# Ten in_b tiles and half of out_even moved between RWKV's matmuls, in plain fp32

## The chip, the core and the metric

One core of one Trainium2 chip runs the whole program. The metric is the device time of one execution in microseconds (us); the median of three runs of the kernel before is 3572.96 us (3570.43 to 3578.23).

## The reference, cut to what matters

The program is one inference step of a two-layer recurrent decoder on T = 320 token columns (a prompt of 256 and eight sequences of 8), D_MODEL = 2048, everything float32. Only layer 0's mixer is touched:

```python
def even_mixer(h, lb, s_hgrn, s_rwkv, s_shift, p, j):
    z = jnp.einsum('btd,de->bte', h, p['w_in_even'][j])       # 2048 x 7424
    z_a, z_b = z[..., :4 * D_A], z[..., 4 * D_A:]             # HGRN2 | RWKV-7
    ...                                                        # o_a: chunked_gated_linear
    prev = jnp.concatenate([s_shift[:, None, :].astype(z_b.dtype), z_b[:, :-1]], axis=1)
    zs = z_b + (prev - z_b) * p['rwkv_mu'][j]                  # token shift
    r, kb, v, wl, al, gl = split_cols(zs, [D_B, D_B, D_B, R_W, R_A, R_G])
    ...                                                        # o_b: rwkv7_scan, group norm, gate
    o = jnp.concatenate([o_a, o_b], axis=-1).astype(h.dtype)
    out = jnp.einsum('bte,ed->btd', o, p['w_out_even'][j])
```

The token shift, and with it all of RWKV, needs the columns z_b; the output projection is a sum over an HGRN half (rows 0 to 1023 of the weights) and an RWKV half.

## The kernel before, in words

Activations lie transposed: 128 features on the partitions, 320 tokens along a row. A projection is a list of tiles of 128 output features; a tile has 16 weight blocks of 128x128, streamed from HBM in two units of eight blocks (512 KB). The order is in_a (32 tiles: HGRN's q, f, i, g), in_b (26 tiles: RWKV's r, k, v and the low-rank inputs), out_even (16 tiles), then the SwiGLU projections and the odd layer, which the change leaves alone.

**Split matmuls.** Every projection is computed in float32r on split operands. ACT rounds a unit's weights to `w_hi` (`split_hi`, L283), DVE or POOL subtracts to get `w_lo` (`split_lo`, L291), and `multiply_unit` (L326) issues three matmuls a block: x_hi and x_lo with w_hi (L348), x_hi with w_lo (L352). The raw weights pass through a ring of four buffers, loaded by SP (`ring_load`, L270), and w_hi and w_lo have two buffers each. In in_b the subtraction is POOL's, elsewhere DVE's.

**HGRN stage.** HGRN2 works through four groups of two heads (`hgrn_act`, `hgrn_dve`, `hgrn_pe`). A group has 21 numbered stages: a head (gates, cumulative log decay), eight levels in which DVE, ACT, PE and DVE hand on to each other (differences L815 and L816, exponentials, products L830 and L831, small Gram matmuls L931 to L937, selects), and a tail (transposes, outputs L957, states L963, sum of squares L974, reciprocal L886, products L981). in_b runs in between: `fill_pe` puts one unit of in_b (24 matmuls) into PE's program at every 1.5 stages, `fill_act` splits and evicts, and `in_b_pool` on POOL subtracts and then applies the token shift to each finished tile (`shift_pool`, nine operations and a memset, L1058 to L1069). `by_stage` (L639) merges such programs by their stage numbers into one program per engine, in which each engine then goes strictly in order.

**RWKV stage.** RWKV-7 runs in two passes; in each, two groups of two head pairs go side by side (`rwkv_act`, `rwkv_dve`, `rwkv_pool`, `rwkv_pe` with x = 0 and 1; buffers in `RwkvBuffers`, L1002). A pass has 74 stages: low-rank projections and norms (0 to 8), transposes and Grams (8 to 16), five rounds of a block-triangular inverse (17 to 36, L1408, L1416, L1418), five chunk steps (37 to 63, L1446 to L1471), the sampled states (65 to 68), group norm and gate (68 to 74). Group x has the PSUM banks 4x to 4x+3. No projection runs beside it.

**out_even.** After the last RWKV group, `mixer_x_act` and `x_lo_dve` split the eight parts of the mixer's output, and out_even runs as 32 units with `evacuate` (L361) and `squares_act` (L407) behind each tile. HGRN's buffers (`hK` and on, L649) lie in the region of M; M held the weighted input `xw` before and takes out_even's result.

Of the kernel before, what the change touches and what calls it, by code (L numbers as in the profile page):

```python
# [17 lines left out]
P = 128  # L18
# [91 lines left out]
def build(nc, d):  # L110
# [5 lines left out]
    with ctx:  # L116
# [126 lines left out]
        FILL = {0: 0, "mix0": 1, 2: 2, 4: 3, "mix1": 4, 6: 5}  # L243
        LEADS, MIXES = {0: 0, 2: 1, 3: 2, 5: 3}, {1: 0, 4: 1}
# [58 lines left out]
        def lead_unit(pe, s, xh, xl, fill):  # L303
# [5 lines left out]
            pe.wait_ge(sem("x_hi"), 8 * fill + c + 1)  # L309
# [16 lines left out]
        def multiply_unit(pe, i, s, xh, xl, fill=None):  # L326
# [9 lines left out]
            half, tile = n % 2, g.tile0 + n // 2  # L336
# [3 lines left out]
            out = PS[tile % 4][:, 0:T]  # L340
            for k in range(g.kt):
                kk = half * g.kt + k
                if fill is not None and not g.lead and n < 2 and kk % 2 == 0:
                    c = kk // 2
                    pe.wait_ge(sem("x_hi"), 8 * fill + c + 1)
                    pe.wait_ge(sem("x_lo_mix"), 8 * MIXES[fill] + c + 1)
# [4 lines left out]
            for k in range(g.kt):  # L351
                mm = nc.tensor.matmul(out, w_lo[s % 2][:, k, :], xh[:, half * g.kt + k, :], start=False,  # L352
                                      stop=half == 1 and k == g.kt - 1)
# [7 lines left out]
        def evacuate(dve, g, out, accumulate=False, stats=None, skip=0, after=None):  # L361
# [19 lines left out]
            def tile_out(i, s):  # L381
# [25 lines left out]
        def squares_act(act, g, stats, w, after, skip=0):  # L407
# [12 lines left out]
            def body(i, s):  # L420
# [3 lines left out]
                if n >= 3 and n % 2:  # L424
                    t = (n - 3) // 2
# [4 lines left out]
            act.activation(warm[:, :], rms_eps, ACT.Sqrt).then_inc(sem("root_table"), 1)  # L430
# [49 lines left out]
        rs = stat[:, 1, :]  # L480

# [12 lines left out]
        def boundary_act(act, n, g, fill, w):  # L494
            if n is not None:
                root_act(act, n)
            for c in range(8):
                if n is None:
                    act.wait_ge(sem(f"x_in{c}"), 16)
# [11 lines left out]
        def boundary_dve(dve, n, g, fill):  # L511
# [5 lines left out]
            for c in range(9):  # L517
# [6 lines left out]
                if c and g is not None:  # L524
                    dve.wait_ge(sem("x_hi"), 8 * fill + c)
# [42 lines left out]
        def mixer_x_act(act):  # L568
            for c in range(8):
# [79 lines left out]
        hK = at("hK", HT0, [P, HG, T])  # L649
        hB = at("hB", HT0 + 2560, [P, HG, T])  # L650
        hEa = at("hEa", HT0 + 5120, [P, HG, T])
        hXa = at("hXa", HT0 + 7680, [P, HG, T])
        hV = at("hV", HT0 + 10240, [P, 3, HG, P])
        hN = at("hN", HT0 + 13312, [P, 3, HG, P])
        att0 = at("att0", HT0 + 16384, [P, HG, 256])
        att1 = at("att1", HT0 + 18432, [P, HG, 128])
        att2 = at("att2", HT0 + 19456, [P, HG, 64])
        hS = at("hS", HT0 + 25728, [P, HG, SEQS, P])
        hVM = at("hVM", HT0 + 19968, [P, SEQS, P])
        hgm_in = at("hgm_in", HT0 + 19968, [P, 8, 128], i32)  # L660
# [31 lines left out]
        def fill_stage(u):  # L692

            return u * (HGROUPS * HSTAGES - 6) // plan["in_b"].units

        def fill_act(act):
            g = plan["in_b"]
            yield 0
            split_hi(act, 0, g.unit0)
            for u in range(g.units + 1):  # L700
                yield fill_stage(u) + (u == g.units)
                if u + 1 < g.units:
                    split_hi(act, 0, g.unit0 + u + 1)
# [1404 lines left out]
```

## Time and profile before

| what | value |
|---|---|
| median of three runs | 3572.96 us |
| the profiled execution's own time | 3568.65 us |
| its span, first to last instruction | 3566.6 us |
| mean granted TensorE clock | 0.957 |
| PE busy, share of the span | 3352.9 us, 94% |
| DVE, ACT, POOL busy | 1917.7, 1253.8, 460.1 us |
| read from HBM | 450.66 MB, 133 GB/s over the span |

Times are from one execution taken by the hardware profiler. "Busy" of PE counts each matmul from its issue to its modelled end, so that matmuls in a pipeline overlap and a busy PE need not be at its peak. A plain fp32 matmul leaves two records, a split one leaves one. The granted clock is 1.00 at 2.4 GHz and 0.50 at 1.2 GHz.

### The profile page before, as it was taken

What the parts mean: (1) busy time and instruction counts of PE and PEld (TensorE: products, weight loads), DVE (VectorE), ACT (ScalarE), POOL (GpSimd) and SP (SyncE); (2) the same over time, 40 slices, a digit from 0 to 9 for tenths busy, and PEclk for the clock granted to TensorE, in tenths of its full rate; (3) what the DMA queues carried; (4) which work ended last, traced back from release to release, by engine and by line L of the source; (5) the groups of instructions that cost most, each with busy time, mean ns of one, the idle gap of its engine ahead of it and who ended that gap; (6) DMA issues with size and microseconds to landing.
All of it is one profiled execution on the core that took longest, in us unless ns stands there. A gap on an engine that the chain in (4) does not pass through costs nothing.

```text
span 3566.6 us, 61189 instructions
## 1 busy us (share of the span) xinstructions
PE 3352.9 (94%) x24672; PEld 3239.9 (91%) x24672; DVE 1917.7 (54%) x2317; ACT 1253.8 (35%) x1582; POOL 460.1 (13%) x400
## 2 busy tenths in 40 slices
PE   8998896858899999999999999998999999999997
PEld 8998885847889999999999899986989999999997
DVE  5446667584566454355544666924475543455444
ACT  5344343232353332233333435321453332233332
POOL 0018774000000000000000035920000000000000
PEclk9999997979899999999999999986999999999999
DMA  6443331000444454454444544533444444445543
GB/s 200 150 143 108 120 108 56 3 26 16 147 131 148 147 150 155 138 151 147 149 159 142 194 147 120 172 137 136 147 130 148 147 154 153 135 147 152 157 146 110
DMA packets 118662, 474.88 MB, mean 133 GB/s; under 512 B 13425, under 2 KB 15089, under 8 KB 115569
## 3 DMA queue, kind: packets, MB, share of 16 engines
q1 hardware_dynamic: 108864, 421.58, 38.4%
q10 hardware_dynamic: 9648, 51.17, 3.7%
q8 instruction: 112, 1.84, 0.2%
q14 instruction: 38, 0.30, 0.0%
HBM read 450.66 MB, written 22.03 MB: 133 GB/s over the span
## 4 chain that ended last, share of the span: by engine, by line
PE 88%; DVE 7%; ACT 2%; issue 1%; POOL 1%; DMA 0%; ACTq 0%; DVEq 0%; POOLq 0%
PE ps L348 49%; PE ps L352 25%; PE ps L1842 1%; PE ps L312 1%; PE ps L317 1%; PE ps L322 1%; PE ps L1862 1%; PE ps L1416 1%; PE ps L957 1%; PE ps L1418 1%; PE ps L1380 0%; PE ps L1365 0%; PE ps L935 0%; PE ps L1597 0%; DVE hEa L886 0%
## 5 line engine op out<-in xcount | busy, mean ns | idle before, releaser
L348 PE MATMUL ps<-x_hi,w_hi 128*128 128x320 f32 x4768 | 1424.1, 312 | 39.9 <-DVE x_lo L548 28.7
L288 ACT ACTIVATE w_hi<-raw 128x1024 fp32r<-128x1024 f32 (+1 forms) x756 | 842.0, 1114 | 1741.3 <-PE ps L352 1688.4
L348 PE MATMUL ps<-x_lo,w_hi 128*128 128x320 f32 x4768 | 1415.6, 310 | 0.0
L296 DVE TENSOR_TENSOR w_lo<-raw,w_hi 128x1024 fp32r<-128x1024 f32 (+1 forms) x640 | 834.5, 1306 | 788.3 <-ACT w_hi L288 775.7
L348 PEld LDWEIGHTS ps<-x_hi,w_hi 128*128 128x128 f32 x4768 | 902.1, 189 | 48.3 <-issue 30.7
L348 PEld LDWEIGHTS ps<-x_lo,w_hi 128*128 128x128 f32 x4768 | 902.1, 189 | 0.9
L352 PE MATMUL ps<-x_hi,w_lo 128*128 128x320 f32 x4768 | 800.9, 310 | 11.4 <-POOL w_lo L296 11.2
L352 PEld LDWEIGHTS ps<-x_hi,w_lo 128*128 128x128 f32 x4768 | 726.1, 189 | 15.2 <-POOL w_lo L296 14.3
L296 POOL TENSOR_TENSOR w_lo<-raw,w_hi 128x1024 fp32r<-128x1024 f32 x116 | 302.8, 2616 | 1682.2 <-ACT w_hi L288 1680.4
L348 PE MATMUL ps<-u_hi,w_hi 128*128 128x320 f32 x1408 | 416.6, 310 | 8.3 <-DVE u_lo L610 8.3
L348 PE MATMUL ps<-u_lo,w_hi 128*128 128x320 f32 x1408 | 416.1, 310 | 0.0
L348 PEld LDWEIGHTS ps<-u_hi,w_hi 128*128 128x128 f32 x1408 | 265.2, 188 | 9.3 <-DVE u_lo L610 9.3
L348 PEld LDWEIGHTS ps<-u_lo,w_hi 128*128 128x128 f32 x1408 | 265.2, 188 | 0.0
L352 PE MATMUL ps<-u_hi,w_lo 128*128 128x320 f32 x1408 | 227.3, 309 | 0.0
L352 PEld LDWEIGHTS ps<-u_hi,w_lo 128*128 128x128 f32 x1408 | 211.7, 188 | 0.0
L601 DVE TENSOR_TENSOR stat<-ps,stat 128x320 f32<-128x320 f32 x88 | 43.3, 492 | 110.3 <-PE ps L352 110.3
L597 DVE TENSOR_TENSOR gate<-ps,stat 128x320 f32<-128x320 f32 x88 | 43.2, 491 | 95.4 <-PE ps L352 95.3
L373 DVE COPY M<-ps 128x320 f32 (+1 forms) x64 | 31.5, 492 | 110.5 <-PE ps L352 110.5
L312 PE MATMUL ps<-x_hi,w_hi 128*128 128x320 f32 x256 | 47.3, 331 | 33.0 <-ACT x_hi L506 33.0
L312 PEld LDWEIGHTS ps<-x_hi,w_hi 128*128 128x128 f32 x256 | 42.4, 205 | 34.4 <-issue 34.4
L371 DVE TENSOR_TENSOR Z<-ps,stat 128x320 f32 (+1 forms) x48 | 22.8, 489 | 52.5 <-PE ps L352 52.5
L369 DVE TENSOR_TENSOR M<-ps,M 128x320 f32 (+1 forms) x32 | 15.7, 492 | 65.3 <-PE ps L352 65.3
(374 smaller groups left out, 2902.9 us busy)
## 6 DMA issues: line engine op xcount, KB each, us to landing
raw<-in_w_ffn_in SPq DMA_DIRECT2D x352, 512.0 KB, 3.6
raw<-in_w_ffn_out SPq DMA_DIRECT2D x128, 704.0 KB, 4.1
raw<-in_w_in_even SPq DMA_DIRECT2D x116, 512.0 KB, 3.6
raw<-in_w_in_odd SPq DMA_DIRECT2D x96, 512.0 KB, 3.6
raw<-in_w_out_even SPq DMA_DIRECT2D x32, 512.0 KB, 3.6
raw<-in_w_out_odd SPq DMA_DIRECT2D x32, 512.0 KB, 3.6
hS<-in_state_hgrn ACTq DMA_DIRECT2D x4, 1024.0 KB, 4.9
out_hgrn_s<-hS ACTq DMA_DIRECT2D x4, 1024.0 KB, 5.1
```

The source lines that it names most:

```text
L288: nc.scalar.activation(w_hi[s % 2][:, 0:g.kt, :], raw[s % 4][:, 0:g.kt, :], ACT.Copy)\
L296: eng.tensor_tensor(w_lo[s % 2][:, 0:g.kt, :], raw[s % 4][:, 0:g.kt, :], w_hi[s % 2][:, 0:g.kt, :].bitcast(f32), sub).then_inc(sem(f"split ...
L312: nc.tensor.matmul(out[t], w_hi[s % 2][:, 4 * kk + t, :], xh[:, 2 * c + kk, :], start=c == kk == 0, stop=False)
L317: nc.tensor.matmul(out[t], w_hi[s % 2][:, 4 * kk + t, :], xl[:, 2 * c + kk, :], start=False, stop=False)
L322: mm = nc.tensor.matmul(out[t], w_lo[s % 2][:, 4 * kk + t, :], xh[:, 2 * c + kk, :], start=False, stop=c == 7 and kk == 1)
L348: nc.tensor.matmul(out, w_hi[s % 2][:, k, :], x[:, kk, :], start=half == 0 and k == 0 and x is xh, stop=False)
L352: mm = nc.tensor.matmul(out, w_lo[s % 2][:, k, :], xh[:, half * g.kt + k, :], start=False, stop=half == 1 and k == g.kt - 1)
L597: dve.tensor_tensor(gate[:, p % 2, :], bank_of(g, 2 * p)[:, 0:T], rs, mult)\
L601: dve.tensor_tensor(uf, bank_of(g, 2 * p + 1)[:, 0:T], rs, mult).then_inc(sem("tile_out"), 1)
L957: ins = mm(o[:, a:a + 8], hS[:, j, b, :], hQ[:, j, 8 * b:8 * b + 8], start=False, stop=b == 7)
L1416: ins = mm(bank[2 + n // 8][a:b, o], r.T1[a:b, n], r.XT[a:b, n], start=True, stop=True)
L1418: ins = mm(bank[n // 8][a:b, o], r.XT[a:b, n], r.T1[a:b, n], start=True, stop=True)
```

## The change

in_b leaves the split scheme. Its 26 tiles are reordered (`IN_B`: those of the first RWKV pass first) and computed as plain fp32 matmuls from the raw weights and the unsplit input `xw`, 16 a tile instead of 48. Sixteen tiles run in the HGRN stage, in chunks of four matmuls; ten run in RWKV's first pass, in chunks of three or four. In RWKV's second pass run the 16 tiles of out_even's HGRN half, eight matmuls each in chunks of 3, 3 and 2, and ACT copies them to M. out_even itself keeps the RWKV half: one unit per tile, added to M. All of this in RWKV uses bank 7, so that group x = 1 has three banks, and some of its rows are cut in two pieces of 192 and 128 columns. The weights of these tiles come through three buffers in the space of the ring, which is loaded again only when the last of them is used. POOL has no weights to split any more; it shifts sixteen tiles in HGRN and ten in RWKV, the latter evicted and scaled by DVE. HGRN's buffers move to the space of x_hi and x_lo, since `xw` has to stay. Smaller parts: the input's eight loads become four, and the subtraction of the mean in RWKV's group norm moves ahead of the state updates on DVE.

```diff
-        dense("in_b", d["w_in_even"], 26, KU_MODEL, "pool", 32)
-        dense("out_even", d["w_out_even"], KT, KU_MODEL, "dve")
+        dense("out_even", d["w_out_even"], KT, KU_MODEL, "dve", 8, 1)
...
             def body(i, s):
                 if s >= 4:
                     split_wait(sp, i, s - 4)
+                if g is plan["out_even"] and s - g.unit0 == 2:
+                    rbuf[1].wait(sp, "ys", 10)
...
+        FILL_H, FILL_B, FILL_O = 16, len(IN_B), KT
+        fraw = [at(f"fraw{i}", RAW0 + 4 * KU_MODEL * P * i, [P, KU_MODEL, P]) for i in range(3)]
+
+        def fill_load(sp):
+            sp.wait_ge(sem("split_lo_dve"), plan["in_a"].units)
+            for u in range(2 * FILL_B + FILL_O):
+                if u >= 3:
+                    sp.wait_ge(sem("fill_unit"), u - 2)
...
+            sp.wait_ge(sem("fill_unit"), 2 * FILL_B + FILL_O)
+
+        def fill_matmul(p, bank, m):
+
+            kt = KU_MODEL
+            u, k = (2 * p + m // kt, m % kt) if p < FILL_B else (FILL_B + p, m)
+            if k == 0:
+                nc.tensor.wait_ge(sem(f"fill_in{u % 3}"), 16 * (u // 3 + 1))
+            last = 2 * kt - 1 if p < FILL_B else kt - 1
+            mm = nc.tensor.matmul(bank, fraw[u % 3][:, k, :], xw[:, m, :] if p < FILL_B else Z[:, m, :],
+                                  start=m == 0, stop=m == last)
...
+        X_IN = (0, 1), (1, 2), (2, 4), (4, 8)
...
-        def fill_stage(u):
-
-            return u * (HGROUPS * HSTAGES - 6) // plan["in_b"].units
+        def fill_stage(p, m):
+
+            return (32 * p + 2 * m) * (HGROUPS * HSTAGES - 2) // (32 * FILL_H)
 
         def fill_act(act):
...
+            for p in range(FILL_H):
+                yield fill_stage(p + 1, 0) + 1
+                fill_done(act, p)
+                act.activation(Z[:, IN_B[p], :], PS[p % 4][:, 0:T], ACT.Copy).then_inc(sem("fill_out"), 1)
 
         def fill_pe(pe):
...
+            for p in range(FILL_H):
+                for m in range(0, 16, 4):
+                    yield fill_stage(p, m)
+                    if m == 0 and p >= 4:
+                        pe.wait_ge(sem("fill_out"), p - 3)
+                    for k in range(m, m + 4):
+                        fill_matmul(p, PS[p % 4][:, 0:T], k)
...
+        def fill_at(p):
+
+            return 6 * (p - FILL_H) if p < FILL_B else RSTAGES + 4.5 * (p - FILL_B)
...
+        def shift_late(pool):
+            for p in range(FILL_H, FILL_B):
+                yield fill_at(p) + 6
+                shift_pool(pool, p)
+
+        def rwkv_fill_pe(pe):
+            for p in range(FILL_H, FILL_B + FILL_O):
+                cuts = (0, 3, 6, 9, 12, 16) if p < FILL_B else (0, 3, 6, 8)
+                for i, (a, b) in enumerate(zip(cuts, cuts[1:])):
+                    yield fill_at(p) + i
+                    if a == 0:
+                        pe.wait_ge(sem("fill_out"), p)
+                    for m in range(a, b):
+                        fill_matmul(p, PS[7][:, 0:T], m)
+
+        def rwkv_fill_dve(dve):
+
+            for p in range(FILL_H, FILL_B):
+                yield fill_at(p) + 5
+                fill_done(dve, p)
+                dve.tensor_tensor(Z[:, IN_B[p], :], PS[7][:, 0:T], rs, mult).then_inc(sem("fill_out"), 1)
+
+        def rwkv_fill_act(act):
+            for p in range(FILL_B, FILL_B + FILL_O):
+                yield fill_at(p) + 3
+                fill_done(act, p)
+                act.activation(M[:, p - FILL_B, :], PS[7][:, 0:T], ACT.Copy).then_inc(sem("fill_out"), 1)
...
-                self.bank = PS[4 * x:4 * x + 4]
+
+                b = self.bank = PS[4 * x:4 * x + (4, 3)[x]]
...
+                    self.row1 = [(b[2][:, T:512], slice(0, 192)), (b[1][:, T:T + 128], slice(192, T))]
...
+                yield at0 + 66
+                w("mu", G + 1)
+                for j in range(RJ):
+                    for ps, ts in r.row(j):
+                        ins = dve.tensor_tensor(r.Y[:, j, ts], r.Y[:, j, ts], ps, sub)
+                ins.then_inc(r.sem("yc"), 1)
                 for j in range(RJ):
                     yield at0 + (66 if j == 0 else 68)
...
-            by_stage(rwkv_act(act, 0), rwkv_act(act, 1))
+            by_stage(rwkv_act(act, 0), rwkv_act(act, 1), rwkv_fill_act(act))
...
-            mixer_x_act(act)
+            mixer_x_act(act, 4)
...
-            by_stage(rwkv_dve(dve, 0), rwkv_dve(dve, 1))
+            by_stage(rwkv_dve(dve, 0), rwkv_dve(dve, 1), rwkv_fill_dve(dve))
...
-            evacuate(dve, plan["out_even"], M, stats=0, skip=HEAD, after=plan["up00"])
+            evacuate(dve, plan["out_even"], M, accumulate=True, stats=0, skip=HEAD, after=plan["up00"])
...
-            by_stage(rwkv_pe(pe, 0), rwkv_pe(pe, 1))
+            by_stage(rwkv_pe(pe, 0), rwkv_pe(pe, 1), rwkv_fill_pe(pe))
```

## Rows read from the trace of the kernel before

**Rows 1.** The chain of work that ended last: shares of the span by engine.
```profile
PE 88%; DVE 7%; ACT 2%; issue 1%; POOL 1%; DMA 0%; ACTq 0%; DVEq 0%; POOLq 0%
```
**Rows 2.** Busy time by stretch (HGRN, RWKV, out_even); columns: length, engines, clock, DMA.
```profile
core 0: us, PE busy (x) PEld busy (x) DVE busy (x) ACT busy (x) POOL busy (x), PEclk, DMA share, GB/s
239.70:586.60 346.90, 309.59 (x1892) 280.06 (x1890) 234.17 (x338) 142.02 (x203) 264.10 (x312) 0.92 0.33 105
586.60:904.90 318.30, 222.30 (x4136) 189.51 (x4136) 201.67 (x326) 84.93 (x191) 6.48 (x4) 0.82 0.06 20
904.90:1022.00 117.10, 112.65 (x750) 112.68 (x751) 58.28 (x70) 51.74 (x72) 0.00 (x0) 0.96 0.53 163
```
**Rows 3.** Timeline of out_even: first matmul of two units in succession.
```profile
915.54 0.31 PE L348 MATMUL ps<-x_hi,w_hi 128*128 128x320 f32 x1
...
919.06 0.31 PE L348 MATMUL ps<-x_hi,w_hi 128*128 128x320 f32 x1
```
**Rows 4.** Chain in order of time: eight fp32 matmuls 128x128x320 in a row.
```profile
2133.58 4.31 PE ps L1597 x16
```
**Rows 5.** Busy time in HGRN: third group's head, levels and tail; the fourth group.
```profile
411.50:429.40 17.90, 14.64 (x92) 14.25 (x90) 5.15 (x10) 13.44 (x17) 10.02 (x13) 0.90 0.69 260
429.40:470.70 41.30, 37.33 (x238) 34.92 (x237) 35.15 (x57) 13.21 (x22) 35.98 (x42) 0.92 0.27 77
470.70:501.60 30.90, 30.06 (x168) 26.31 (x167) 17.06 (x16) 9.86 (x16) 23.48 (x30) 0.89 0.31 88
501.60:586.60 85.00, 71.44 (x413) 61.52 (x411) 57.65 (x83) 31.33 (x46) 62.78 (x85) 0.86 0.27 88
```
**Rows 6.** Timeline of DVE in the third group's levels.
```profile
433.67 2.52 DVE L815 TENSOR_TENSOR hEa<-hB 128x320 f32<-128x320 f32 x1
436.11 2.66 DVE L816 TENSOR_TENSOR hEa<-hB 128x320 f32<-128x320 f32 x1
...
455.93 0.41 DVE L815 TENSOR_TENSOR hEa<-hB 128x256 f32<-128x256 f32 x1
```
**Rows 7.** Timeline of POOL at the same time.
```profile
432.79 5.63 POOL L296 TENSOR_TENSOR w_lo<-raw,w_hi 128x1024 fp32r<-128x1024 f32 x2
```
**Rows 8.** Timeline of PE in the third group: one level, then the tail.
```profile
456.99 1.05 PE L935 MATMUL ps<-hXa 128*128 128x128 f32 x8
...
477.08 2.59 PE L957 MATMUL ps<-hQ,hS 128*128 128x8 f32 x16
...
485.70 1.98 PE L963 MATMUL ps<-hVM,hN 64*128 64x512 f32 x4
...
491.23 1.24 PE L974 MATMUL ps<-Z,com 128*128 128x320 f32 x4
```
**Rows 9.** Busy time in RWKV's first pass, and the end of the second.
```profile
591.70:621.50 29.80, 10.36 (x32) 5.81 (x32) 25.06 (x34) 12.68 (x22) 3.21 (x2) 0.61 0.09 30
621.50:645.90 24.40, 19.63 (x300) 18.70 (x300) 20.19 (x38) 7.78 (x20) 0.00 (x0) 0.92 0.01 1
645.90:684.50 38.60, 33.84 (x994) 33.17 (x995) 22.38 (x38) 6.65 (x14) 0.00 (x0) 0.87 0.01 4
684.50:713.00 28.50, 26.85 (x618) 25.77 (x619) 4.75 (x15) 6.95 (x26) 0.00 (x0) 0.95 0.01 3
713.00:747.00 34.00, 21.25 (x140) 11.76 (x137) 26.22 (x34) 5.96 (x12) 0.00 (x0) 0.80 0.14 51
...
869.00:904.90 35.90, 19.51 (x141) 11.25 (x140) 27.21 (x36) 6.04 (x12) 0.00 (x0) 0.79 0.09 34
```
**Rows 10.** Timeline of PE in RWKV: two groups of four small matmuls at clock 1.00.
```profile
664.27 0.33 PE L1418 MATMUL ps<-T,XT 64*64 64x64 f32 x4
...
664.39 0.33 PE L1416 MATMUL ps<-XT,T 64*64 64x64 f32 x4
```
**Rows 11.** Timeline of POOL: first and last of one tile's ten shift instructions.
```profile
475.08 0.85 POOL L1058 TENSOR_TENSOR Z<-Z,stat 128x320 f32<-128x320 f32 x1
...
478.46 0.86 POOL L1069 TENSOR_TENSOR Z<-Z,shd 128x320 f32<-128x320 f32 x1
```

More of the change, by code:

```diff
@@ L335, in multiply_unit @@
             pe.wait_ge(sem("split_hi"), i * 8 + (s + 1))
-            half, tile = n % 2, g.tile0 + n // 2
+            half, tile = (n % 2, g.tile0 + n // 2) if g.parts == 2 else (0, g.tile0 + n)
             if half == 0 and tile >= 4 and not (g.lead and n < 14):
@@ L340, in multiply_unit @@
             out = PS[tile % 4][:, 0:T]
+            k0 = half * g.kt if g.parts == 2 else g.kt
             for k in range(g.kt):
[L342 to L346, printed above, removed]
+                kk = k0 + k
+                if fill is not None and not g.lead and n < g.parts and kk % 2 == 0:
+                    c = kk // 2 if g.parts == 2 else k // 2
+                    pe.wait_ge(sem("x_hi"), fill + c + 1)
+                    pe.wait_ge(sem("x_lo_mix"), MIXES[fill] + c + 1)
                 for x in (xh, xl):
@@ L351, in multiply_unit @@
             for k in range(g.kt):
-                mm = nc.tensor.matmul(out, w_lo[s % 2][:, k, :], xh[:, half * g.kt + k, :], start=False,
-                                      stop=half == 1 and k == g.kt - 1)
+                mm = nc.tensor.matmul(out, w_lo[s % 2][:, k, :], xh[:, k0 + k, :], start=False,
+                                      stop=half == g.parts - 1 and k == g.kt - 1)
             mm.then_inc(sem("unit_done"), 1)
@@ L388, in tile_out @@
                         one(0, t, g.unit0 + 2 * t + 2)
+                elif g.parts == 1:
+                    one(0, n, s + 1)
                 elif n % 2 and not (g.lead and n < 12):
@@ L566, in mixer_part, with mixer_x_act @@
             return Z[:, z:z + 2, :]
-        def mixer_x_act(act):
-            for c in range(8):
+        def mixer_x_act(act, first=0):
+            for c in range(first, 8):
                 act.activation(part(x_hi, c), mixer_part(c), ACT.Copy).then_inc(sem("x_hi"), 1)
@@ L1395, in rwkv_pe @@
                 w("gm", 5 * G + 3)
-                gram(4, 2, bank[2]).then_inc(r.sem("n4"), 1)
+                for c in range(4 if x else 0):
+                    ins = gram(c, 2, r.n03[:, 64 * RJ * c:64 * RJ * c + 64 * RJ])
+                    if c == 3:
+                        ins.then_inc(r.sem("n03"), 1)
+                if x:
+                    w("gm", 5 * G + 4)
+                gram(4, 2, r.n4).then_inc(r.sem("n4"), 1)
                 for l in range(1, 6):
@@ L1893, in _ @@
             for name in ORDER:
+                if name == "out_even":
+                    fill_load(sp)
                 ring_load(sp, plan[name])
@@ L2054 @@
     w_odd_units = units(np.concatenate([qk, w_odd[:, 2048:]], axis=1), KU_MODEL)
+    in_even, out_even = units(a["w_in_even"][0], KU_MODEL), units(a["w_out_even"][0], KU_MODEL)
+    in_b = [b + j for b in (R_B, K_B, V_B) for j in range(4)] + [WA_B, GL_B] + \
+           [b + j for j in range(4, 8) for b in (R_B, K_B, V_B)]
+    in_even = np.concatenate([in_even[:64]] + [in_even[2 * t:2 * t + 2] for t in in_b])
     dram = {
```

248 lines of the change are left out of this document (137 added, 111 removed).

## Prediction

> **What bounds the kernel now.** I read the chain of waits first: PE's share of it is 88% [rows 1], so what counts is how long PE's program takes, its own waiting included. Then the busy time by stage [rows 2]: the change touches three stages, HGRN with in_b (346.9 us), RWKV (318.3 us) and out_even (117.1 us). out_even is PE without a gap. In HGRN all of PE, DVE and POOL are busy over two thirds of the time; in RWKV PE shows 222 of 318 us at a mean granted clock of 0.82, and nothing but RWKV's own chain runs there. Then the pace of the two kinds of matmul. A split unit of 24 matmuls takes 919.06 - 915.54 = 3.52 us [rows 3], 0.147 us each and 0.440 us for the three that a weight block needs. Eight plain fp32 matmuls of the same shape (16 records) take 4.31 us [rows 4], 0.539 us each. So fp32 is dearer for PE by 0.099 us a block, and cheaper only for those who split.
>
> PE's work by these paces: in_b 416 blocks x 0.440 = 183.0 us and out_even 256 x 0.440 = 112.6 us before; after it 256 x 0.539 = 138.0 us in HGRN, (160 + 128) x 0.539 = 155.2 us in RWKV and 128 x 0.440 = 56.3 us in out_even. PE gets 54 us more work. The change wins only if RWKV hides much of its 155 us and HGRN shrinks by the lighter load.
>
> **HGRN.** A middle group takes 90 us: head 17.9, levels 41.3, tail 30.9 [rows 5]. Its fills were 13 units, 45.8 us of PE; they become 4 tiles, 34.5 us, in chunks of 4 x 0.539 = 2.16 us instead of units of 3.52 us.
>
> Levels. DVE's six large operations of a level take 0.41 us each where nothing disturbs them, 2.5 us a level; but single ones show 2.5 to 2.7 us [rows 6], for as long as POOL's subtractions of w_lo run [rows 7]. Those are gone with the change. A level's Gram takes PE 1.05 us [rows 8]; with a handover I take 1.2. A stage with a chunk then costs 2.16 + 1.2 + 0.1 = 3.4 us, one without is DVE's 2.5; there are 64 chunks in 82 stages, so 0.78 x 3.4 + 0.22 x 2.5 = 3.2 us a stage. The first three levels also carry the sequences: 3.7. That is 5 x 3.2 + 3 x 3.7 + 3 for the ends = 30, with 1.5 for POOL's shifts 31.5: 9.8 us less than now. The same sum with a unit of 3.52 us at two stages of three gives 37 of the 41 seen; the rest is POOL.
>
> Tail. From the end of the outputs L957 at 479.7, units stand ahead of L963 (485.70) and L974 (491.23) [rows 8]; the first ran at half clock. Chunks there instead shorten 21.8 us to about 17.2: 4.6 us less. The head is DMA and table loads; I take 0.5 us off for the split that ACT no longer does. So two middle groups gain 14.9, the first, with a shorter head, 13; the last, whose tail had hardly any fill (85.0 us), 9.5: **HGRN -52 us**. If DVE and PE still wait for each other at every stage, a group gains only 6, 24 us in all; if the stalls all go and chunks fall into DVE's time, 20, 80 us in all.
>
> **RWKV.** Own sum by window [rows 9], chunks by the stage numbers in the diff; a chunk of three is 1.62 us, an in_b tile 8.62 us.
> - 591.7 to 621.5 (stages 0 to 8): 11.9 us of chunks, PE idle 19.4: DVE is the bound. Hidden but for the chunk ahead of the first low-rank matmuls, 3.2 us at half clock, and an eviction: +4.
> - 621.5 to 645.9: 14.0 us of chunks, 4.8 idle, 1 back from the clock (0.92 granted; the chunks keep PE at it): +8.
> - 645.9 to 684.5, the inverse: 27.5 us of chunks, 4.8 idle, and 4 back from the clock (0.87: 10 us at half): +18.7.
> - 684.5 to 713, the chunk steps: 32.9 us of chunks. PE shows 26.85 busy of 28.5, but four records take 664.39 - 664.27 = 0.12 us [rows 10], so 618 records are 18.5 us of work and the rest their latency. Between 1.7 and 10 us idle I take 7, nearer the pace since the two groups alternate: +25.9.
> - 713 to 747: no chunks. The mean is subtracted before the state updates: -2.
>
> First pass +54.6. The second pass has windows within 2 us of these and 16 tiles of 4.31 us, 69.0 us, spread to stage 144: 8.6, 8.6, 18.9, 21.6 and 11.3 us by window, of which I hide 7.6, 5.1, 8, 6 and 10 (the last window's PE is idle for 16.4): +32. Unseen costs: PE's change between 64x64 and full tiles at 98 chunks (0 to 0.25 us each, a handover like the 0.1 above); x = 1 with three banks (four more ACT or DVE pieces a pass, 0 to 0.4 us each; no gain but the -2 above); ten shifts on POOL beside RWKV's DVE. I take +5 for them together, near the low end, since most fall where PE has other work. **RWKV +92 us**, so 155 - 92 = 63 us hidden. From below: all idle of the windows used, +75; from above: only the DVE-bound windows at the starts of the passes hide anything, 155 - 20 - 10 of clock = +125.
>
> New waits. PE waits for bank 7's eviction before each tile; queued behind are all RWKV matmuls. In the first window that eviction stands on DVE behind two long reciprocals, but so do the transposes. ACT's 16 copies and DVE's 10 evictions (0.4 to 0.5 us) wait for chunks that PE runs before what they need next. SP's loads are 84 units of 512 KB before and after; three buffers leave two units (8.6 us) for a landing. The four merged input loads are covered by the 20 us before their last parts are used; uncovered, some us once.
>
> **out_even** loses 384 split matmuls: -56 us (54 to 58). DVE's add to M costs what its copy did; two tiles instead of one finish behind the last unit, below 1 us.
>
> **Sum:** -52 + 92 - 56 = -16 us. The sum is against the profiled execution, 3568.65 us, which lies 4.3 below the median shown, 3572.96; I forecast the median: **3557 us**.
>
> **The rivals.**
> - *Forecast*, 0.45: RWKV +82 to +100, HGRN -45 to -60; 3540 to 3570, within 0.2% of before in a fifth of it. (0.2%, 7 us, is about what a measurement of this kernel can tell from no change.)
> - *HGRN was held by POOL*, 0.24: POOL is busy for 36 of the levels' 41 us [rows 5]; without its lock-outs and with finer chunks a group goes to 70 us. HGRN -80: 3529. Against it: the last group lost four units of fill and gained only 5 us.
> - *A chunk is a step of RWKV's chain*, 0.16, slower: PE goes strictly in order, so both groups' next step stands behind each chunk even where DVE or ACT would have been waited for anyway only for a moment; from the inverse on nothing is hidden. RWKV +125: 3573 + 17 = 3590. It decides once RWKV grows by more than 52 + 56 = 108 us. For it: PE shows 27 of 28.5 us in the chunk steps. Against: the pace in rows 10.
> - *POOL locks DVE out in RWKV*, 0.06, slower: a shift takes 479.3 - 475.1 = 4.2 us [rows 11], 3.4 without its first operation; ten of them are 34 us beside a DVE that is the bound in three windows. All of it on the path: -16 + 34 - 2 = +16, 3589. In HGRN's levels DVE's 35.2 busy us exceed its undisturbed 24 by 11, a third of POOL's 36, which would make it 10. The Trainium skill (SBUF — State Buffer, "SBUF: two separate sides") has a rule for this: GpSimd and a VectorE operation with two SBUF inputs share a port pair as an exclusive lock, and the loser waits out the whole instruction. By that rule the full 34 us could come due; the trace agrees that a stalled operation ends with POOL's, and shows that most meet none.
> - *HGRN does not shrink*, 0.05, slower: its chain of handovers, not the fills, sets the pace, so the lighter load does nothing. -20 instead of -52: 3589.
> - *A wash*, 0.04: the errors cancel; 3573.
>
> **How the numbers follow.** Faster: 0.36 of the forecast and the second case, 0.60. Same: 0.09 + 0.04 + 0.03 from the edges of the slower ones, 0.16. Slower: 0.24. The range goes from somewhat below the second case (RWKV a little better with it) to just above 3590: 3515 to 3592. The likeliest case's own range is 3540 to 3570.
>
> **What would show it.** Right: HGRN's groups at 74 to 77 us, DVE operations in the levels at 0.4 to 0.5 us; RWKV at 400 to 415 us with PE's clock near 1.00 from the transposes to the chunk steps; out_even's matmuls half as many in half the time. Wrong: groups still at 85 us; RWKV over 425 us, with DVE and ACT waiting for PE at every step of the inverse and the chunk steps; DVE operations of 1 us beside POOL's shifts on the chain; PE waiting for bank 7 or for a weight load.

## The result: 0.46% slower, and the profile after

The changed kernel takes 3589.84 us (median of seven runs, 3583.56 to 3596.86), the kernel before 3573.35 beside it: 1.0046 times as long, 95% interval 1.0033 to 1.0059. One of the seven runs of the kernel before, 4055.29 us, was slow and does not enter the ratio. The forecast was 3557 and faster; the time lies inside the range, on the wrong side.

The profiled execution took 3584.75 us, 16.1 more than that of before. I cut both traces at marks that both kernels have (first moved matmul, last mark of HGRN, last write of RWKV's gate, first transpose and end of the odd layer's retention stage); times in us:

| stretch | before | after | predicted | measured |
|---|---|---|---|---|
| to the first in_b matmul | 240.2 | 238.5 | 0 | -1.7 |
| HGRN | 346.5 | 280.4 | -52 | -66.1 |
| RWKV | 318.1 | 448.1 | +92 | +130.0 |
| out_even, up to the retention stage | 1438.4 | 1383.0 | -56 | -55.4 |
| retention stage (code not touched) | 139.2 | 148.4 | 0 | +9.2 |
| from there to the end | 1084.3 | 1084.7 | 0 | +0.4 |

So up to the retention stage the change comes to +6.8 (-1.7 of it ahead of HGRN), 0.2% of the time; between a second profile of each kernel, below, it is +3.6. The larger part of the 16.1 is a stage 1400 us later. The same stretches by busy time (HGRN, RWKV, out_even), which answer to [rows 2]:

```profile
core 0: us, PE busy (x) PEld busy (x) DVE busy (x) ACT busy (x) POOL busy (x), PEclk, DMA share, GB/s
238.00:518.80 280.80, 259.24 (x1152) 185.84 (x1152) 166.51 (x338) 89.13 (x142) 73.02 (x150) 0.92 0.29 93
518.80:967.00 448.20, 389.54 (x4728) 294.40 (x4728) 209.89 (x341) 92.05 (x210) 47.20 (x104) 0.90 0.19 58
967.00:1030.60 63.60, 58.54 (x384) 58.31 (x384) 37.47 (x53) 32.73 (x52) 0.00 (x0) 0.93 0.55 176
```

HGRN's POOL time fell from 264 to 73 us and its DVE time from 234 to 167 us. In RWKV PE is busy for 167 us more, DVE and ACT for 8 and 7 each, POOL for 41: the 130 us are PE's, or POOL's by way of DVE.

**HGRN after.** DVE's timeline in a level of the third group, against [rows 6]: nothing of 2.5 us is left.

```profile
402.22 0.41 DVE L858 TENSOR_TENSOR hEa<-hB 128x256 f32<-128x256 f32 x1
402.56 0.41 DVE L859 TENSOR_TENSOR hEa<-hB 128x256 f32<-128x256 f32 x1
```

PE's timeline in the same levels: a chunk and a Gram follow each other without a gap, 412.29 - 409.24 = 3.05 us a stage. In these levels PE now sets the pace.

```profile
409.24 2.32 PE L310 MATMUL ps<-M,fraw 128*128 128x320 f32 x8
411.40 1.05 PE L978 MATMUL ps<-Z 128*128 128x128 f32 x8
412.29 2.32 PE L310 MATMUL ps<-M,fraw 128*128 128x320 f32 x8
```

**RWKV after.** Busy time by stage: start, transposes and Grams, inverse, chunk steps with the sampled state, end; the first pass, then the second. Read the PE column against the length: in rows 2 to 4 and 7 to 9 PE is busy for 94% or more, at the starts and ends of the passes for half to two thirds.

```profile
518.90:557.70 38.80, 24.55 (x80) 16.00 (x80) 28.30 (x40) 16.74 (x28) 11.75 (x21) 0.74 0.26 85
557.70:594.00 36.30, 34.31 (x352) 27.90 (x352) 23.00 (x41) 7.68 (x20) 3.80 (x10) 0.95 0.15 45
594.00:655.30 61.30, 60.21 (x1095) 48.53 (x1094) 23.53 (x41) 6.64 (x14) 14.11 (x36) 1.00 0.20 62
655.30:724.60 69.30, 69.04 (x811) 53.62 (x810) 7.45 (x21) 8.32 (x30) 12.06 (x35) 0.93 0.22 63
724.60:754.20 29.60, 18.57 (x74) 8.99 (x74) 26.51 (x37) 4.55 (x7) 2.26 (x3) 0.88 0.16 56
754.20:783.30 29.10, 16.53 (x54) 10.62 (x54) 26.38 (x40) 14.87 (x26) 3.22 (x2) 0.73 0.20 58
783.30:813.70 30.40, 29.48 (x334) 24.89 (x334) 20.19 (x38) 8.56 (x22) 0.00 (x0) 0.92 0.06 19
813.70:869.40 55.70, 52.91 (x1064) 43.41 (x1064) 23.04 (x39) 8.40 (x18) 0.00 (x0) 0.97 0.17 50
869.40:933.40 64.00, 63.84 (x793) 49.72 (x792) 6.97 (x20) 10.79 (x36) 0.00 (x0) 0.92 0.15 45
933.40:967.00 33.60, 20.12 (x81) 10.72 (x80) 24.45 (x32) 5.41 (x9) 0.00 (x0) 0.83 0.25 94
```

PE's timeline at the first chunk step shows how: two groups' products of 0.6 us stand between runs of six and seven moved matmuls. Six matmuls hold PE for 659.35 - 655.92 = 3.43 us, against 6 x 0.539 = 3.23 back to back: 0.2 a run for the change between small and full tiles. The Trainium skill (TensorEngine Tiling (Array Packing), "Key Properties") says that changing the tiling mode drains the engine; these rows agree in that 0.2 us a run is lost, though no row shows a drain itself.

```profile
655.31 0.68 PE L1563 MATMUL ps<-nat,G 64*64 64x64 f32 x16
655.92 3.50 PE L310 MATMUL ps<-M,fraw 128*128 128x320 f32 x12
659.35 0.68 PE L1573 MATMUL ps<-RH,XT 64*64 64x64 f32 x16
659.96 4.04 PE L310 MATMUL ps<-M,fraw 128*128 128x320 f32 x14
```

### The profile page after: what moved, and what is told of

It is laid out like the page before. It is cut to its first block, busy times and chain, and to the rows that moved or that the text cites. A ratio compares the mean times of both kernels' runs of the same rounds, so it can differ in the third digit from the quotient of the medians.

```text
span 3583.0 us, 59330 instructions
## 1 busy us (share of the span) xinstructions
PE 3423.4 (96%) x24144; PEld 3198.2 (89%) x24144; DVE 1835.8 (51%) x2313; ACT 1188.1 (33%) x1518; POOL 308.7 (9%) x338
## 4 chain that ended last, share of the span: by engine, by line
PE 91%; DVE 6%; ACT 2%; DMA 1%; issue 1%; ACTq 0%; SPq 0%; DVEq 0%
PE ps L390 46%; PE ps L394 23%; PE ps L310 7%; PE ps L1966 1%; PE ps L1986 1%; PE ps L352 1%; PE ps L357 1%; PE ps L362 1%; PE ps L978 1%; PE ps L1533 1%; PE ps L1525 1%; PE ps L1490 1%; PE ps L1721 0%; PE ps L1553 0%; PE ps L1535 0%
## 5 line engine op out<-in xcount | busy, mean ns | idle before, releaser
L390 PE MATMUL ps<-x_hi,w_hi 128*128 128x320 f32 x4224 | 1252.4, 310 | 28.7 <-DVE x_lo L595 27.0
L390 PE MATMUL ps<-x_lo,w_hi 128*128 128x320 f32 x4224 | 1249.7, 309 | 0.0
L390 PEld LDWEIGHTS ps<-x_hi,w_hi 128*128 128x128 f32 x4224 | 794.9, 188 | 32.2 <-issue 28.7
L390 PEld LDWEIGHTS ps<-x_lo,w_hi 128*128 128x128 f32 x4224 | 795.0, 188 | 0.6
L394 PE MATMUL ps<-x_hi,w_lo 128*128 128x320 f32 x4224 | 706.2, 309 | 0.4 <-DVE w_lo L336 0.3
L394 PEld LDWEIGHTS ps<-x_hi,w_lo 128*128 128x128 f32 x4224 | 641.0, 188 | 2.9 <-POOL w_lo L336 1.7
L336 POOL TENSOR_TENSOR w_lo<-raw,w_hi 128x1024 fp32r<-128x1024 f32 x64 | 169.8, 2659 | 1380.3 <-ACT w_hi L328 1380.3
L310 PE MATMUL ps<-M,fraw 128*128 128x320 f32 x832 | 265.0, 470 | 15.5 <-DVE Z L1165 9.8
L310 PEld LDWEIGHTS ps<-M,fraw 128*128 128x128 f32 x832 | 164.5, 205 | 85.7 <-issue 23.7
L310 PE MATMUL ps<-Z,fraw 128*128 128x320 f32 x256 | 81.7, 464 | 0.0
L352 PE MATMUL ps<-x_hi,w_hi 128*128 128x320 f32 x256 | 47.3, 331 | 31.5 <-ACT x_hi L553 31.5
L352 PEld LDWEIGHTS ps<-x_hi,w_hi 128*128 128x128 f32 x256 | 42.4, 205 | 32.9 <-issue 32.9
```

Source lines behind the costliest of these rows:

```text
L310: mm = nc.tensor.matmul(bank, fraw[u % 3][:, k, :], xw[:, m, :] if p < FILL_B else Z[:, m, :], start=m == 0, stop=m == last)
L336: eng.tensor_tensor(w_lo[s % 2][:, 0:g.kt, :], raw[s % 4][:, 0:g.kt, :], w_hi[s % 2][:, 0:g.kt, :].bitcast(f32), sub).then_inc(sem(f"split ...
L352: nc.tensor.matmul(out[t], w_hi[s % 2][:, 4 * kk + t, :], xh[:, 2 * c + kk, :], start=c == kk == 0, stop=False)
L390: nc.tensor.matmul(out, w_hi[s % 2][:, k, :], x[:, kk, :], start=half == 0 and k == 0 and x is xh, stop=False)
L394: mm = nc.tensor.matmul(out, w_lo[s % 2][:, k, :], xh[:, k0 + k, :], start=False, stop=half == g.parts - 1 and k == g.kt - 1)
```

## The experiments

Theory "PE pays": work moved between RWKV's matmuls is free only where PE waited for DVE; elsewhere each matmul costs its 0.54 us and each run of them its change of tile. Rivals: side costs of the move (three banks, evictions, POOL), pieces that delay the chain, and POOL as what held HGRN.

**All of in_b left in HGRN (`e4_hgrn26`).**

```diff
-        FILL_H, FILL_B, FILL_O = 16, len(IN_B), KT
+        FILL_H, FILL_B, FILL_O = len(IN_B), len(IN_B), KT
```

> All 26 tiles of in_b run in HGRN, still in plain fp32 and chunks of four; RWKV's first pass has none; out_even's half stays in the second pass. 'PE pays': HGRN is bound by PE too now, ten tiles of 8.62 us add 75 to 85 us to its 281 (355 to 366), and RWKV's first pass gives back about 80: 3580 to 3600 in all. Rival 'HGRN has room': with POOL's subtractions gone the tiles fall into PE's waits there, HGRN 330 to 345 and the time 3560 to 3575.

Measured: 3567.12 us, 0.9985 (0.9976 to 0.9995) of before. Both HGRN's 337.6 us and the time lie in the range of the rival 'HGRN has room'; 'PE pays' had HGRN at 355 or more. Ten tiles of 86 us add 57, so HGRN hides 29 of them. Its busy time:

```profile
239.60:577.20 337.60, 336.56 (x1472) 244.53 (x1472) 170.34 (x339) 92.72 (x152) 121.13 (x250) 0.96 0.34 108
```

PE's idle time there fell from 21.6 us (280.80 - 259.24) to 1.0, and at a mean granted clock of 0.96 in place of 0.92 some 9 us less are lost (0.08 x 280.8 against 0.04 x 337.6, an estimate): together these are the 29. So the room was PE's own idle time and its clock, and the idle time is used up. RWKV's first pass, now without tiles and still with seven banks:

```profile
577.20:611.30 34.10, 11.69 (x37) 7.53 (x37) 27.01 (x40) 16.90 (x28) 7.32 (x12) 0.68 0.19 66
611.30:636.30 25.00, 20.75 (x302) 19.25 (x302) 20.18 (x38) 7.68 (x20) 0.00 (x0) 0.89 0.01 2
636.30:673.80 37.50, 32.13 (x992) 31.46 (x992) 22.32 (x38) 6.64 (x14) 0.00 (x0) 0.91 0.01 3
673.80:707.50 33.70, 32.05 (x691) 30.84 (x689) 6.43 (x18) 8.37 (x30) 0.00 (x0) 0.87 0.03 7
707.50:737.50 30.00, 19.53 (x80) 9.57 (x76) 25.48 (x37) 4.54 (x7) 0.00 (x0) 0.84 0.15 53
```

The sum is 160.3 us, 161.3 before: the missing fourth bank, the cut rows and the moved mean together cost nothing. Against the changed kernel's first five rows this prices the moved matmuls stage by stage (their count is half the records of L310 in the stretch; a matmul on a boundary counts on both sides, and the three at the end are out_even's):

| stage | without | with | matmuls x 0.539 | cost | predicted |
|---|---|---|---|---|---|
| start | 34.1 | 38.8 | 22: 11.9 | 4.7 | 4 |
| transposes, Grams | 25.0 | 36.3 | 26: 14.0 | 11.3 | 8 |
| inverse | 37.5 | 61.3 | 52: 27.8 | 23.8 | 18.7 |
| chunk steps | 33.7 | 69.3 | 62: 33.2 | 35.6 | 25.9 |
| end | 30.0 | 29.6 | 3: 1.6 | -0.4 | -2 |

In all 75 us, where leaving the ten tiles in HGRN costs 57: the move of the ten tiles loses 18.

**Only the HGRN part**, out_even whole behind RWKV.

```diff
-        FILL_H, FILL_B, FILL_O = 16, len(IN_B), KT
+        FILL_H, FILL_B, FILL_O = len(IN_B), len(IN_B), 0
...
-        dense("out_even", d["w_out_even"], KT, KU_MODEL, "dve", 8, 1)
+        dense("out_even", d["w_out_even"], KT, KU_MODEL, "dve")
...
```

Its out_even reads the weight units in the order in which the changed kernel stores them, by halves, and multiplies them tile by tile, so the layer's output is another sum; the amount of work is that of before.

> Only the HGRN part of the change: all 26 tiles of in_b in plain fp32 in HGRN, nothing between RWKV's matmuls (seven banks stay), out_even whole behind it as before. 'The move is what lost': HGRN 338 as in e4_hgrn26 against 347 before, RWKV 315 to 320, out_even 119 to 121; no slower than the kernel before: 3560 to 3566 with a retention stage of 139 us, 3569 to 3575 with one of 148. 'Plain fp32 is what lost' (a weight block takes PE 0.54 us instead of 0.44): slower than the kernel before, 3580 or more.

Measured: 3552.08 us, 0.9945 (0.9928 to 0.9963); HGRN 334.2, RWKV 313.8, the time below both ranges of 'The move is what lost'. Plain fp32 in HGRN is not what lost: it gains 12 us there although each block costs PE more. Single runs spread from 3543.9 to 3568.6, and the profiled one was the slowest, with a retention stage of 156 us.

**out_even's half only where PE waited.**

In `o_tile` stand a tile's place in PE's program, its bank, the place of ACT's copy and what has to be done with the bank before:

```diff
+        def o_tile(q):
+            G, i = divmod(q - 1, 8)
+            at0 = G * RSTAGES
+            if q == 0:
+                return 0.5, 7, 1.0, None
+            if i < 5:
+                return at0 + 4.2 + i / 10, (7, 0, 1, 4, 7)[i], at0 + (5.5, 6.5, 6.6, 6.7, 8.6)[i], \
+                    (None, (0, "norm"), (0, "norm"), (1, "norm"), None)[i]
+            return at0 + 72 + (i - 5) / 10, (0, 1, 7)[i - 5], at0 + 72 + (i - 5) / 10, \
+                ((0, "sd"), (0, "sd"), None)[i - 5]
...
```

> All of in_b in HGRN as in e4_hgrn26, and out_even's sixteen HGRN-half tiles not spread over RWKV's second pass but set where PE waited in the passes without fills: one before the first low-rank products, five ahead of the transposes and three (two in the second pass) behind the gate of each pass, over the free banks 7, 0, 1 and 4. 'PE pays': a moved matmul is free only where PE waits; the trace of the first pass of e4_hgrn26 shows waits of 5, 17, 7, 5 and 3 us, some 60 us in both passes for 69 us of work. RWKV 327 to 337 instead of 372, the time 3522 to 3532. Rival 'the pieces delay the chains around them': ACT's copies between the exponentials and the low-rank products behind the tiles make each of the four clusters 5 us or more longer than its matmuls' excess: RWKV 350 or more, 3545 or more.

Measured: 3510.32 us (five runs, 3509.32 to 3517.16), 0.9833 (0.9820 to 0.9846): faster than both kernels. RWKV takes 318.0 us, as long as before and 4 us longer than without any moved work (313.8), with all 69 us of out_even's half in it; 327 to 337 were expected. PE's timeline ahead of the transposes: five tiles as one run of 40 matmuls, 0.54 us each.

```profile
591.09 21.70 PE L310 MATMUL ps<-Z,fraw 128*128 128x320 f32 x80
612.63 0.60 PE L1499 MATMUL ps<-com,Z 128*64 128x128 f32 x4
```

and busy time of the first two stages, which answer to the first two rows of the kernel with all in_b in HGRN above:

```profile
574.30:612.60 38.30, 33.81 (x132) 23.25 (x133) 30.14 (x44) 18.64 (x33) 7.35 (x12) 1.00 0.40 130
612.60:635.00 22.40, 18.19 (x301) 17.55 (x299) 17.09 (x31) 8.00 (x21) 0.00 (x0) 0.98 0.09 26
```

The start is 4.2 us longer, since the tiles are more than its waits hold. The transposes and Grams behind it are 2.6 us shorter, at a granted clock of 0.98 in place of 0.89; but most of this is not the clock. DVE's first copy of a transpose, here and in the kernel with all in_b in HGRN:

```profile
613.70 2.61 DVE L1292 COPY nat<-ps 64x256 f32<-64x256 f32 x6 [2.54 <-PE ps L1499]
```

```profile
614.38 1.72 DVE L1268 COPY nat<-ps 64x256 f32<-64x256 f32 x4
```

It comes 1.1 us after the first transpose (612.63) here and 3.1 us after it (611.3) there, where DVE first finishes some 3 us of the second group's products, which the longer start takes over here. That is 2.0 of the 2.6 us.

**An eighth of the moved matmuls.**

```diff
                     for m in range(a, b):
-                        fill_matmul(p, PS[7][:, 0:T], m)
+                        if m % KU_MODEL == KU_MODEL - 1:
+                            fill_matmul(p, PS[7][:, 0:T], m)
...
```

In `fill_matmul` the wait for a unit's weights and the start of a sum move to the matmul that is left.

> Leaves out seven eighths of the moved products in RWKV (one matmul of every eight stays, with its loads, evictions, shifts and the seven banks), so ten in_b tiles and half of out_even are not what they should be. Theory 'PE pays': from the transposes on PE has no time to spare, so every moved matmul costs its 0.54 us, every change between small and full tiles some 0.19 us, and only the waits for DVE at the ends of a pass hide any. Then RWKV falls from 448 us to 318 to 330, and the time to 3462 to 3478. Theory 'side costs': 30 us or more of RWKV's growth come from group x = 1 with three banks, the evictions and POOL's shifts. Then RWKV stays at 345 to 360 and the time at 3490 to 3505. For both: the retention stage, whose code is the same, moves by up to 10 us with the clock granted there.

Measured: 3477.86 us (four runs, 3464.50 to 3492.12), the upper end of the first theory's range; RWKV 339.8, between the two. The first pass without tiles above has settled the banks, so what stays is the pieces: this first pass takes 174.3 us with 20 lone matmuls against 160.3 without, 0.70 us each, which is 0.54 and 0.16 for the change of tile; the second pass gives 0.71 (165.6 with 16, 154.2 in the kernel with only the HGRN part). Even lone matmuls, spread evenly, are not hidden. My figure for the first theory had left these out.

**One piece a tile.**

```diff
-                cuts = (0, 3, 6, 9, 12, 16) if p < FILL_B else (0, 3, 6, 8)
+                cuts = (0, 16) if p < FILL_B else (0, 8)
```

> Every moved tile runs in RWKV as one piece (16 or 8 matmuls) instead of five or three: 26 pieces instead of 98, which stand as 64 uninterrupted runs in the trace. 'PE pays': same matmuls, fewer changes of tile shape, 38 x 0.19 = 7 us less, with a few us of hiding lost: 3580 to 3592. Rival 'a piece is a delay of the chain of both groups': pieces of 4 to 8.6 us in place of 1.6 make each group wait longer than PE could use: 3605 or more.

Measured: 3601.99 us, 1.0088 (1.0071 to 1.0104); RWKV 458.8, 10.7 longer, between the two figures. The first pass's start alone went from 38.8 to 50.8 us. PE's timeline there:

```profile
522.94 11.71 PE L310 MATMUL ps<-M,fraw 128*128 128x320 f32 x32 [5.05 <-ACT Z L1179]
...
558.91 10.82 PE L310 MATMUL ps<-M,fraw 128*128 128x320 f32 x32 [11.55 <-DVE Z L1165]
569.57 1.26 PE L1475 MATMUL ps<-com,Z 128*64 128x128 f32 x10
```

One whole tile, partly at half clock, stands ahead of the low-rank products, where three matmuls do in the changed kernel; the next waits 11.55 us for DVE to empty bank 7 and then stands whole ahead of the transposes. The chunk steps, with fewer pieces, fell from 69.3 to 59.1, the inverse rose from 61.3 to 73.2, together 132.3 against 130.6: there the size of a piece hardly matters.

**RWKV's shifts left out**, but for the two copies of the shift state.

```diff
             if p < FILL_H:
                 L(pool.tensor_tensor(z, z, rs, mult))
+            else:
+                pool.tensor_copy(sh_out[:, n, 0:1], z[:, 255:256])
+                pool.tensor_copy(sh_out[:, n, 1:9], z[:, 263:T:8]).then_inc(sem("shifted"), 1)
+                pool.wait_ge(sem("shifted"), p + 1)
+                return
```

> Leaves out seven of the nine POOL operations of the ten token shifts in RWKV (only the two copies for the shift state stay), so RWKV's second pass works on unshifted columns. 'PE pays': PE sets the pace, DVE's waits behind POOL cost little: 0 to 5 us less, 3585 to 3590. Rival 'POOL locks DVE out in RWKV': ten shifts of about 3 us each come off the path: 25 to 30 us less, 3560 to 3565.

Measured: 3590.11 us, 1.0052 (1.0033 to 1.0070), the same as the changed kernel. RWKV is 3.5 us shorter (444.6), and the retention stage of the profiled run 7.6 longer. That is inside the first theory's 0 to 5. So POOL's shifts have next to no part in RWKV's growth.

**POOL's load put back in HGRN, and taken out of the kernel before.** In the first, `xf` are columns of `xw` and `load_to` is unused space.

```diff
             pool.wait_ge(sem("fill_out"), p + 1)
+            for _ in range(3 if p < FILL_H else 0):
+                L(pool.tensor_tensor(load_to[:, :], xf[:, 0:1024], xf[:, 1024:2048], sub))
```

> The changed kernel with the load on POOL put back in HGRN: three subtractions of 128x1024 for each of the sixteen tiles, on data that nobody uses, some 125 us of POOL in all. 'POOL held HGRN': DVE operations of 2.5 us come back, and HGRN grows from 281 to 300 to 315 us. 'PE pays': PE sets the pace in the levels, DVE has slack for the stalls: HGRN 281 to 290.

Measured: 3642.95 us, 1.0197 (1.0182 to 1.0211); HGRN 335.6 instead of 280.4, beyond the ranges of both theories. DVE's timeline in a level, and POOL's beside it:

```profile
445.00 2.50 DVE L858 TENSOR_TENSOR Z<-hB 128x256 f32<-128x256 f32 x1
447.43 2.56 DVE L859 TENSOR_TENSOR Z<-hB 128x256 f32<-128x256 f32 x1
449.92 2.56 DVE L873 TENSOR_TENSOR hXa<-hK,hEa 128x256 f32<-128x256 f32 x1
```

```profile
444.88 7.32 POOL L1127 TENSOR_TENSOR load_to<-M 128x1024 f32<-128x1024 f32 x3 [9.76 <-ACT Z L747]
```

Three DVE operations of 0.41 us take 2.5 each, one for each of POOL's three, and each ends 0.2 to 0.3 us behind it. The Trainium skill (SBUF — State Buffer, "SBUF: two separate sides") says that the loser of the port pair waits out the whole instruction of the other; these rows agree, 2.44 us (7.32 / 3) being one POOL operation.

The kernel before, with POOL's subtraction cut to one block of eight:

```diff
-            eng.tensor_tensor(w_lo[s % 2][:, 0:g.kt, :], raw[s % 4][:, 0:g.kt, :],
-                              w_hi[s % 2][:, 0:g.kt, :].bitcast(f32), sub).then_inc(sem(f"split_lo_{name}"), 1)
+            kt = 1 if g is plan["in_b"] else g.kt
+            eng.tensor_tensor(w_lo[s % 2][:, 0:kt, :], raw[s % 4][:, 0:kt, :],
+                              w_hi[s % 2][:, 0:kt, :].bitcast(f32), sub).then_inc(sem(f"split_lo_{name}"), 1)
```

> The kernel before, with POOL's subtraction of w_lo in in_b cut to the first of its eight weight blocks, so seven eighths of in_b's low weight parts are stale and its result is not exact; PE, ACT and DVE issue the same instructions as before. 52 operations of 2.7 us become short, some 120 us less of POOL. 'POOL held HGRN': HGRN falls from 347 us to 305 to 320. 'PE pays': PE's own 310 busy us and the handovers set the pace, HGRN 335 to 345.

Measured: 3541.63 us, 0.9905 (0.9888 to 0.9922); HGRN 323.2 instead of 346.5, between the two. So seven eighths of POOL's subtraction cost the kernel before 23 us. Why about the same load costs 55 in the changed kernel, where three operations come in a row, no run settles.

**The retention stage.** Four runs: each kernel again, and each with the stage's first four transposes issued seven times.

```diff
-                for k in range(4):
+                for k in [0, 1, 2, 3] * (7 if m == 0 else 1):
```

> The kernel before, unchanged, for a second profile. If the clock in the retention stage goes with the program, that stage takes 139 us again and the whole 3566 to 3571. If it changes from run to run, the stage takes 148 or 156 us as in the five other profiles, and the time of this run is longer by as much.

> The changed kernel, unchanged, for a second profile: layer 0's mixer within 1 us of the first, and a retention stage of 148 or 156 us. A stage of 139 us would say that the clock there changes from run to run and that the changed kernel has no part in it; the time would then be 3575 to 3578.

> The kernel before, with the first four transposes of the retention stage issued seven times instead of once, 24 x 0.114 = 2.7 us more PE work at the start of the stage and nothing else. 'The stage's place decides which part of it meets the full clock': the stage takes 148 us or more, the time 3581 or more. 'The programs ahead of it decide': 139 + 3 = 142 us, 3575 to 3577.

> The same 2.7 us of repeated transposes in the changed kernel. 'The stage's place decides': its length leaves 148 + 3 by 8 us or more either way. 'The programs ahead of it decide': 151 us, the time 3 us longer than the changed kernel's.

Measured: before again 139.1 us (3574.3 in all), after again 148.4 (3587.19; layer 0's mixer 1.4 us longer than in the first profile). With the 2.7 us of transposes: the kernel before takes 3588.50 us, 1.0037 (1.0027 to 1.0048), its stage 152.9; the changed kernel 3580.45, 1.0020 (1.0010 to 1.0031) of before and 9 us below its own median, its stage 145.9 in the profiled run, which is 2 us shorter than the changed kernel's. The first answers as 'the stage's place' had it; the second lies 5.5 us from the 151 of the other theory, short of the 8 us asked, and fits neither. Busy time of the whole stage, before and after, then cut where the granted clock changes; the kernel before, the changed one, and the longest stretch at half clock of the one before with the transposes:

```profile
2343.10:2482.30 139.20, 129.22 (x512) 92.51 (x512) 53.48 (x70) 24.26 (x44) 0.87 (x1) 0.70 0.29 113
```

```profile
2349.90:2498.30 148.40, 138.41 (x513) 96.10 (x513) 53.55 (x70) 24.32 (x45) 0.83 (x1) 0.65 0.27 106
```

```profile
2343.10:2359.10 16.00, 15.14 (x112) 13.72 (x112) 6.51 (x13) 11.03 (x21) 0.87 (x1) 0.99 0.45 157
2359.10:2376.10 17.00, 17.00 (x70) 15.80 (x69) 0.00 (x0) 0.77 (x2) 0.00 (x0) 0.50 0.24 100
2376.10:2390.10 14.00, 14.00 (x58) 7.81 (x57) 9.50 (x10) 2.41 (x3) 0.00 (x0) 0.98 0.24 99
2390.10:2403.10 13.00, 13.00 (x49) 11.44 (x49) 1.97 (x4) 0.77 (x2) 0.00 (x0) 0.50 0.56 217
2403.10:2417.10 14.00, 14.00 (x59) 7.90 (x59) 9.57 (x10) 1.12 (x2) 0.00 (x0) 0.99 0.26 109
...
2430.10:2444.10 14.00, 14.00 (x59) 7.89 (x60) 9.63 (x10) 0.97 (x2) 0.00 (x0) 0.98 0.26 111
```

```profile
2349.90:2368.90 19.00, 18.18 (x136) 16.66 (x137) 6.51 (x13) 11.03 (x21) 0.83 (x1) 0.99 0.54 204
2368.90:2419.90 51.00, 51.00 (x150) 36.23 (x150) 11.47 (x13) 4.54 (x8) 0.00 (x0) 0.50 0.22 89
2419.90:2432.90 13.00, 13.00 (x56) 7.23 (x54) 9.21 (x10) 0.53 (x1) 0.00 (x0) 1.00 0.24 101
2432.90:2446.90 14.00, 14.00 (x53) 11.78 (x53) 2.27 (x4) 1.36 (x3) 0.00 (x0) 0.52 0.14 57
2446.90:2460.90 14.00, 14.00 (x62) 8.24 (x60) 10.23 (x12) 0.53 (x1) 0.00 (x0) 0.99 0.31 131
```

```profile
2399.60:2450.60 51.00, 51.00 (x151) 36.32 (x150) 13.07 (x16) 3.17 (x7) 0.00 (x0) 0.50 0.23 93
```

Length times granted clock is 97.4 and 96.5 us (139.2 x 0.70, 148.4 x 0.65), so the clock accounts for the difference. In the stretches at half clock PE is busy all through, on the stage's many short products. The clock drops to 1.2 GHz 16 to 19 us into it and comes back to 2.4 GHz for spells of 13 to 14 us: three in the kernel before, two in the other two, which stay at half for 51 us at a stretch. A lost spell costs about 9 us here (148.4 - 139.2), and with the transposes 152.9 - 139.2 - 2.7 = 11. So 2.7 us of the stage's own work make the kernel before 16 us slower, as much as the whole change does, and by the medians the changed kernel faster. What fixes which spells a kernel gets stays open. Of the fourteen profiles, three have 139 us (the kernel before twice, and with POOL's load cut), seven 148 to 149 (the changed kernel twice, and five of its variants), two 156 (its variants without shifts and with the HGRN part alone), and the two with the transposes lie elsewhere. The stages of 139 us have three spells of full clock behind the first drop, those of 148 to 149 two, those of 156 one.

## Why the prediction was wrong

**RWKV is the step that failed.** Its +92 measured +130. "155 - 92 = 63 us hidden" was summed from PE's idle time, window by window [rows 9]; 25 were hidden (155 - 130). At the start and the end of the first pass the terms held, and less was hidden at each stage between. In the chunk steps "Between 1.7 and 10 us idle I take 7, nearer the pace since the two groups alternate" failed outright: nothing was hidden, and the cost, 35.6, exceeds the matmuls' own 33.2 by twelve changes of tile. The step in error is to take the pace of [rows 10], 0.03 us a record in the inverse, as PE's need in the chunk steps and all beyond it as room. The trace of before already shows otherwise. All that PE waits for there (684.5 to 717.2), by releaser, and two marks of its timeline, with twenty matmuls between them:

```profile
PE ps L1446 <- DVE ST L1273: 0.6, 2, 0.3
PE ps L1446 <- DVE XT L1258: 0.5, 1, 0.5
```

```profile
691.31 0.22 PE L1470 MATMUL ps<-SA,nat 64*64 64x64 f32 x1
...
692.12 0.22 PE L1470 MATMUL ps<-SA,nat 64*64 64x64 f32 x1
```

PE waits 1.1 us for other engines, and between the marks its products start 0.04 us apart (0.81 / 20). By that pace the stage's 688 records are some 28 of its 32.7 us, an estimate, where 18.5 of 28.5 had been taken. With the moved matmuls the stage's own products still take 31.6 of the 69.3 us, and the twelve runs 37.7. PE's program left little room. That the size of a piece changes nothing in the inverse and the chunk steps (132.3 against 130.6) fits this better than a delay behind each piece. The second pass failed at the same place: 15.6 (21.6 less 6) became 29.9 (64.0 against 34.1 between the same marks of before), partly because more of out_even's pieces came to lie there (51 matmuls, 27.7 us, where 21.6 us were taken).

**The change of tile** was bounded at 0 to 0.25 us a chunk, a bound that no row gave, and taken near zero. It is 0.19 a run, and some 64 runs make 12 us, where +5 was to cover it together with banks and shifts. Of those, the banks with the moved mean cost nothing and the shifts 3.5 us.

**HGRN** was right in direction and too small: -52 measured -66. Groups take 68 to 69 us, the last 74, against 74 to 77 expected. A stage with a chunk is 3.05 us, not 3.4. The rival "HGRN was held by POOL" had the mechanism, and the two POOL runs show it, but not its -80. The larger part of the -66 is lighter load: putting the ten tiles back costs 57 of it.

**out_even** was right: -56 predicted, -55.4 measured.

**What no step contained** is the retention stage: +9.2 of the 16.1 us between the two profiled executions, from the granted clock. What fixes the clock's pattern there stays open.

**The rivals.** "A chunk is a step of RWKV's chain" came true nearly in its size (+125): from the inverse on next to nothing was hidden. Its reason, that a chunk delays the chain however short the wait it fills, is less well borne out than that PE's own program left little room: larger pieces cost no more there. That its total, 3590, is the measured one is chance: HGRN gave 14 us more than in its sum, the retention stage took 9 back and RWKV 5. "POOL locks DVE out in RWKV" and "HGRN does not shrink" fell.

## What to carry to other kernels

Give an in-order engine extra work inside a wait that the trace names, with its length, and not evenly by stage number: the same sixteen tiles cost 56 us spread over a pass and 4 us or less in the gaps. Take what an engine needs from the stage itself, and not from the densest pace elsewhere. Before moving elementwise work to GpSimd, see whether VectorE's chain beside it has operations with two SBUF inputs, and before believing a difference of half a percent, compare the stages whose code is the same.

## What was not expected of the hardware

A stage whose code and load are the same takes 139 to 156 us by which spells of full clock it meets, with PE busy throughout. The pattern came back in a second profile of each kernel (139.2 and 139.1, 148.4 and 148.4), so that comparing medians does not remove it, while 2.7 us of extra work changed it. Other kernels seem to meet several patterns: the six times of the one with the HGRN part alone lie at 3544, 3551 to 3553 and 3567 to 3569, though only one of the six was profiled.
